# x also loaded turned, its first norm's factors applied after the product, and the first w_in slabs taken in a new order

## The chip, the cores and the metric

One Trainium2 chip, one core. The metric is the device time of one launch in microseconds. The kernel before takes 1186.05 us, the median of three runs (1185.82 to 1186.39).

## The reference

Two transformer blocks in a row on 512 tokens of width 1024, in float32. The change touches the start of the first: the first norm, the product with w_in, the norms of the heads.

```python
def rmsnorm(x, g):
    x32 = x.astype(jnp.float32)
    y = x32 * lax.rsqrt(jnp.mean(x32 * x32, axis=-1, keepdims=True) + EPS)
    return (y * g.astype(jnp.float32)).astype(x.dtype)
...
        xn = rmsnorm(x, attn_norm_g)
        proj = jnp.einsum('bsd,de->bse', xn, w_in)
        qa, ka, va, qb, kb, vb, f_logit = jnp.split(proj, IN_SPLITS, axis=-1)
        qa = rmsnorm(qa.reshape(b, s, A_HEADS, HEAD_DIM), q_norm_a)
        ka = rmsnorm(ka.reshape(b, s, A_KV_HEADS, HEAD_DIM), k_norm_a)
        out_a = swa_sinks_attention(qa, ka, va, sink_logits)
        ...
        out_b = forgetting_attention(qb, kb, vb, log_f)
        x = x + jnp.einsum('bse,ed->bsd', mixed, w_out)
        hn = rmsnorm(x, mlp_norm_g)
        hid = jnp.square(jax.nn.relu(jnp.einsum('bsd,df->bsf', hn, w_up)))
        x = x + jnp.einsum('bsf,fd->bsd', hid, w_down)
```

The second block (modulated norms, a pooling mixer, neighbourhood attention, a second MLP) follows and isn't changed.

## The kernel before

The code is written by engine: every engine's queue is an order set by hand, and semaphores join the queues. An engine does its instructions strictly in that order, so whatever stands behind a waiting one waits too.

**Products.** A float32 operand is split in a high part (rounded to fp32r) and a low part (the rest). A product is three matmuls for each of 8 blocks k of the inner dimension: high with high, high with low, low with high (`passes`, L1091 to L1093). xt_hi and xt_lo hold x turned: 128 partitions of the inner dimension, 8 blocks k, 512 tokens.

**Weights.** w_in is taken in five slabs (`IN1_COLS`): slab 0 is q of mixer a (512 columns), slab 1 its k and v and the forget logits (256 + 8 columns, in two loads, L512 and L513), slabs 2 to 4 are q, k, v of mixer b. A slab comes in four units q of two blocks k, 512 KB each, into raw[q] (the load on SP's queue, `unit`, L471); ScalarE writes the high part (`high`, L606), VectorE the low part (`low`, L1707), counted in hi_split and unit_split. A unit's load for the next slab waits until unit_split says that raw[q] was read. A slab's split also waits (`slab_end`) until the slab two before is used up.

**The start.** SP loads x tile 0 (128 tokens, 512 KB), unit 0 of slab 0, the identity, then units and x tiles in turn, then slab 1 with 17 small loads among it. TensorE spreads the norm's gain over the partitions by two products with a row of ones (L1148), then turns tile 0 of x times gain (`turn_half`, L1132, four turns each). The root of the mean square of tile 0 is late: it is applied behind the product (`root0`, `late_root`). Tiles 1 to 3 are scaled by root and gain first (`first_rows`, `scaled`, L1686), then turned; ScalarE copies the turns as xt_hi (`xt_high`, L636), VectorE subtracts for xt_lo (`xt_low`, L1697). ScalarE also does x's squares (`first_squares`, L620) and roots (`first_root`, L625, L626), VectorE the mean and refining (L1667, L1674, L1675).

**The order of tiles.** `FIRST` lists eight products (slab, row tile) g = 0 to 7 in the banks gp[g % 4]. `first_product` is the first, unit by unit; the others go through `product`, with turns put in their middle by `between(g)`. From g = 4 on a product waits until gp[g % 4] is free.

```python
FIRST = ((0, 0), (0, 1), (0, 2), (1, 0), (1, 1), (1, 2), (1, 3), (0, 3))
```

**The heads.** For each g: ScalarE squares the product (`head_squares`, L675), VectorE reduces it by heads (`head_means`, L1735, L1737), ScalarE takes two steps of the root (`head_roots`, L682, L683), VectorE refines it (`refine_heads`, L1660 to L1662) and writes the normed heads qn (`head_rows`, L1750 or L1751), which frees the bank (gemm_free). TensorE turns qn (`turn_heads`, L1207), and ScalarE stores q or k times gain (`head_gain`, L661, counted in qk_stored). For slab 1 ScalarE also copies v_a and flog (L718, L719). `sinks` (VectorE, L1776 to L1783) makes the sinks' rows from a small load.

**Behind it** runs a loop over `HALVES1` = 70 halves: attention of pairs of heads (`scores`, L1275; `maxima`, L1857; `exps`, L735; `turn_probs`; `copy_probs`; `values`) between three blocks k at a time of the products with slabs 2 to 4 (`part_product`). scores(0) waits for gemm_free 6, the small loads, the sinks and qk_stored 4 (k of tile 0); turn_probs(0), behind scores(1), waits for the exps of scores(0). Slab 2 is split by ScalarE around g = 6 and 7, since it takes the place of slab 1.

Of the kernel before, what the change touches and what calls it, by code (L numbers as in the profile page):

```python
# [14 lines left out]
P = 128  # L15
# [34 lines left out]
FIRST = ((0, 0), (0, 1), (0, 2), (1, 0), (1, 1), (1, 2), (1, 3), (0, 3))  # L50
N_IN1, N_OUT, N_MLP, N_IN2 = 5, 2, 4 * NCH, 4
# [188 lines left out]
def build(nc, t, out):  # L240
    ctx = ExitStack()
    with ctx:
# [50 lines left out]
        gain_row = at("gain_row", [1, D], F32, H + 28 * K)  # L293
        ones_row = at("ones_row", [1, P], F32, H + 20 * K)
# [37 lines left out]
        gains = place("gains", [P, 4], F32)  # L332
        cvec = place("cvec", [P, 2, KT], F32)
# [14 lines left out]
        gain1 = at("gain1", [P, D], F32, E)  # L348
# [38 lines left out]
        def sem(name):  # L387
# [70 lines left out]
        def _(sp):  # L458
# [5 lines left out]

            x_tile(0)
# [10 lines left out]
            def slab(s, w, c0, width):  # L476
                for q in range(UQ):
                    wait = 4 * (s - 1) + q + 1 if s else None
                    unit(q, rows(w, 0, q)[:, :, c0:c0 + width], width, wait)
                    if s == 0 and q == 0:  # L480
                        small(ident[:], t["c_ident"], ident_loaded)
                    if s == 0 and q:
                        x_tile(q)

            for s, (c0, width) in enumerate(IN1_COLS):
                if s == 1:

                    small_loads = (
                        (gains[0:HD, 0:1], t["q_norm_a"].rearrange("(p a) -> p a", a=1), heads_loaded),
                        (gains[HD:P, 0:1], t["q_norm_a"].rearrange("(p a) -> p a", a=1), heads_loaded),  # L490
                        (gains[0:HD, 1:2], t["k_norm_a"].rearrange("(p a) -> p a", a=1), heads_loaded),
                        (gains[HD:P, 1:2], t["k_norm_a"].rearrange("(p a) -> p a", a=1), heads_loaded),
                        (gains[0:HD, 2:3], t["q_norm_b"].rearrange("(p a) -> p a", a=1), heads_loaded),
                        (gains[HD:P, 2:3], t["q_norm_b"].rearrange("(p a) -> p a", a=1), heads_loaded),
                        (gains[0:HD, 3:4], t["k_norm_b"].rearrange("(p a) -> p a", a=1), heads_loaded),
                        (gains[HD:P, 3:4], t["k_norm_b"].rearrange("(p a) -> p a", a=1), heads_loaded),
                        (b_f[:], t["b_forget"].rearrange("(p a) -> p a", a=1), vec_loaded),
                        (sink[:], t["sink_logits"].rearrange("(a n) -> a n", a=1), vec_loaded),
                        (cvec[:, 0, :], t["c"], vec_loaded),
                        (cvec[:, 1, :], t["c_ctx"], vec_loaded),  # L500
                        (identb[:], t["c_identb"], vec_loaded),
                        (causal[:], t["c_causal"], vec_loaded),
                        (edge[:], t["c_edge"], vec_loaded),
# [3 lines left out]
                    for q in range(UQ):  # L507
                        src = rows(t["w_in"], 0, q)
                        for args in small_loads[5 * q:5 * (q + 1)]:
                            small(*args)  # L510
# [1934 lines left out]
```

## Time and profile before

| | |
|---|---|
| median of the runs | 1186.05 us (1185.82 to 1186.39) |
| the profiled execution | 1186.4 us, of which its span 1184.5 us |
| TensorE busy | 1167.0 us, 99% |
| VectorE, ScalarE, GpSimd busy | 706.3 us (60%), 476.1 us (40%), 24.8 us (2%) |
| TensorE clock granted | 0.998 of full speed, mean |
| DMA | 144.28 MB, mean 122 GB/s |

PE is TensorE's matmuls, PEld its weight loads, DVE is VectorE, ACT is ScalarE, SPq and ACTq are DMA issues by SyncE and ScalarE. A timeline's row gives the start in us from the span's start, the duration in us, engine, line, operation, tile written <- tiles read, shapes, count, and in square brackets how long the engine had been idle and what ended that. The ends of matmuls are modelled, so starts are what to read there. The chain of work that ended last is followed back from the last instruction.

### The profile page before, as it was taken

How to read it: one execution, taken by the hardware profiler on the slowest of the kernel's cores; microseconds unless marked ns; L12 is line 12 of the kernel's file. 1: busy time of each engine (PE TensorE's matmuls, PEld its weight loads, DVE VectorE, ACT ScalarE, POOL GpSimd, SP SyncE). 2: the span in 40 equal slices, each digit the busy share in tenths (PEclk: the TensorE clock that was granted, in tenths of full speed). 3: DMA queues.
4: the chain of work that ended last, by engine and by line, in shares of the span. 5: the costliest groups of instructions: out<-in, count | busy, mean ns of one | idle time of the engine just before them, and what ended most of it. 6: DMA issues, size and time to landing. Idle time of an engine off the chain costs nothing.

```text
span 1184.5 us, 16596 instructions
## 1 busy us (share of the span) xinstructions
PE 1167.0 (99%) x6158; PEld 946.1 (80%) x6160; DVE 706.3 (60%) x1084; ACT 476.1 (40%) x858; POOL 24.8 (2%) x23
## 2 busy tenths in 40 slices
PE   8999999989999999999999999999999999999997
PEld 5877776688888888888888886678988888888886
DVE  7786567768787786842788235747633333324335
ACT  6655344545234234324541114845631532432431
POOL 0000000000000000000000004300000000000000
PEclk9999999999999999999999999999999999999999
DMA  7322211218766676734425111222333322323301
GB/s 229 125 72 71 72 36 54 73 52 271 243 224 242 215 254 206 232 125 142 143 72 171 72 72 46 80 101 72 128 99 96 105 91 89 110 85 99 117 16 71
DMA packets 77533, 144.28 MB, mean 122 GB/s; under 512 B 8339, under 2 KB 12307, under 8 KB 77460
## 3 DMA queue, kind: packets, MB, share of 16 engines
q1 hardware_dynamic: 54882, 99.12, 24.7%
q10 hardware_dynamic: 22578, 44.18, 11.4%
q8 instruction: 46, 0.75, 0.3%
q14 instruction: 27, 0.22, 0.1%
HBM read 140.36 MB, written 2.13 MB: 120 GB/s over the span
## 4 chain that ended last, share of the span: by engine, by line
PE 91%; DVE 5%; ACT 2%; issue 2%; DMA 0%; DVEq 0%; ACTq 0%
PE gemm L1091 26%; PE gemm L1093 25%; PE gemm L1092 25%; PE aux L1132 1%; PE aux L1338 1%; PE gemm L1378 1%; PE gemm L1380 1%; PE gemm L1379 1%; DVE nmax L2199 1%; PE aux L1091 1%; PE gemm L1275 1%; PE aux L1093 1%; PE aux L1092 1%; PE gemm L1288 1%; PE aux L1617 1%
## 5 line engine op out<-in xcount | busy, mean ns | idle before, releaser
L1091 PE MATMUL gemm<-xt_hi,w_hi 128*128 128x512 f32 (+1 forms) x704 | 254.4, 361 | 1.3 <-issue 1.1
L1093 PE MATMUL gemm<-xt_hi,w_lo 128*128 128x512 f32 (+1 forms) x704 | 253.6, 360 | 0.0
L1092 PE MATMUL gemm<-xt_lo,w_hi 128*128 128x512 f32 (+1 forms) x704 | 253.5, 360 | 0.0
L1707 DVE TENSOR_TENSOR w_lo<-w_raw,w_hi 128x1024 fp32r<-128x1024 f32 (+1 forms) x176 | 208.0, 1210 | 35.1 <-ACT w_hi L842 30.4
L842 ACT ACTIVATE w_hi<-w_raw 128x1024 fp32r<-128x1024 f32 x124 | 124.1, 1050 | 211.4 <-PE gemm L1093 132.9
L1091 PE MATMUL gemm<-w_hi,ht_hi 128*128 128x512 f32 (+1 forms) x512 | 198.9, 388 | 0.0
L1093 PE MATMUL gemm<-w_hi,ht_lo 128*128 128x512 f32 (+1 forms) x512 | 198.4, 387 | 0.0
L1092 PE MATMUL gemm<-w_lo,ht_hi 128*128 128x512 f32 (+1 forms) x512 | 198.4, 387 | 0.0
L1091 PEld LDWEIGHTS gemm<-xt_hi,w_hi 128*128 128x128 f32 x704 | 132.7, 188 | 21.9 <-issue 1.7
L1093 PEld LDWEIGHTS gemm<-xt_hi,w_lo 128*128 128x128 f32 x704 | 132.7, 189 | 20.1
L1092 PEld LDWEIGHTS gemm<-xt_lo,w_hi 128*128 128x128 f32 x704 | 132.7, 188 | 19.8
L2005 DVE TENSOR_TENSOR ht_lo<-hid,ht_hi 128x512 fp32r<-128x512 f32 x64 | 44.3, 692 | 162.4 <-ACT hid L855 162.4
L1093 PEld LDWEIGHTS gemm<-w_hi,ht_lo 128*128 128x128 f32 x512 | 96.1, 188 | 19.7
L1092 PEld LDWEIGHTS gemm<-w_lo,ht_hi 128*128 128x128 f32 x512 | 96.2, 188 | 19.5
L1091 PEld LDWEIGHTS gemm<-w_hi,ht_hi 128*128 128x128 f32 x512 | 96.1, 188 | 19.4
L850 ACT ACTIVATE relu<-gemm 128x512 f32<-128x512 f32 x64 | 38.2, 597 | 165.3 <-PE gemm L1093 160.2
L2062 DVE SCALAR_TENSOR_TENSOR mod_acc<-wm,csil,mod_acc 128x512 f32<-128x512 f32 x112 | 84.1, 751 | 5.8 <-DMA wm<-in_w_mod 1.5
L1091 PE MATMUL gemm<-w_hi,xt_hi 128*128 128x512 f32 (+1 forms) x208 | 80.2, 386 | 0.4 <-DVE xt_lo L1697 0.4
L1093 PE MATMUL gemm<-w_hi,xt_lo 128*128 128x512 f32 (+1 forms) x208 | 77.9, 374 | 0.0
L1092 PE MATMUL gemm<-w_lo,xt_hi 128*128 128x512 f32 (+1 forms) x208 | 77.6, 373 | 0.0
L606 ACT ACTIVATE w_hi<-w_raw 128x1024 fp32r<-128x1024 f32 (+1 forms) x52 | 51.0, 1021 | 61.1 <-PE gemm L1093 60.0
L2019 DVE TENSOR_TENSOR sub<-sub,gemm 128x512 f32<-128x512 f32 (+1 forms) x24 | 16.2, 676 | 60.5 <-PE gemm L1093 60.5
(268 smaller groups left out, 1385.8 us busy)
## 6 DMA issues: line engine op xcount, KB each, us to landing
wm<-in_w_mod ACTq DMA_DIRECT2D x64, 512.0 KB, 4.7
w_raw<-in_w_in SPq DMA_DIRECT2D x32, 512.0 KB, 4.3
w_raw<-in_w_up SPq DMA_DIRECT2D x32, 512.0 KB, 3.9
w_raw<-in_w_down SPq DMA_DIRECT2D x32, 512.0 KB, 5.7
w_raw<-in_w_mlp_in SPq DMA_DIRECT2D x32, 512.0 KB, 3.6
w_raw<-in_w_mlp_out SPq DMA_DIRECT2D x32, 512.0 KB, 4.4
w_raw<-in_w_out SPq DMA_DIRECT2D x16, 512.0 KB, 4.0
x<-in_x SPq DMA_DIRECT2D x4, 512.0 KB, 6.5
```

The lines of the kernel that those rows point to most:

```text
L606: act.activation(w_hi[slot(s)][:, UK * q:UK * (q + 1), 0:width], raw[q][:, :, 0:width], ACT.Copy).then_inc(hi_split, 1)
L842: act.activation(w_hi[s % 2][:, UK * q:UK * (q + 1), :], raw[q][:, :, :], ACT.Copy).then_inc(hi_split, 1)
L850: act.activation(relu[c % 2][:], gp[(t0 + c) % 4][:], ACT.Relu).then_inc(relu_done, 1)
L1091: pe.matmul(bank, lh, rh, start=(k == 0), stop=False)
L1092: pe.matmul(bank, lh, rl, start=False, stop=False)
L1093: mm = pe.matmul(bank, ll, rh, start=False, stop=(k == KT - 1))
L1132: mm = pe.transpose(dst, src, ident[:])
L1275: pe.matmul(bank[e][:, lo:256], q_a[rows[e], h // 2, n * P:(n + 1) * P], k_a[rows[e], swap, (n - 1) * P + lo:(n + 1) * P], start=True, sto ...
L1707: dve.tensor_tensor(w_lo[slot(s)][:, ks, 0:width], raw[q][:, :, 0:width], w_hi[slot(s)][:, ks, 0:width].bitcast(F32), ALU.subtract).then_i ...
L2005: dve.tensor_tensor(ht_lo[:, c, :], hid[c % 2][:], ht_hi[:, c, :].bitcast(F32), ALU.subtract).then_inc(hid_lo, 1)
L2019: dve.tensor_tensor(cols, cols, bank[:], ALU.add).then_inc(gemm_free, 1)
L2062: ins = dve.scalar_tensor_tensor(acc, w, c, acc, ALU.mult, ALU.add)
```

## The change

The host lays x out once more, turned (`x_turned`, 8 blocks k of 128 partitions x 512 tokens), the norm's gain by partition, the head gains in one array and the two conditioning vectors in one. In the kernel:

- The gain products, the turns of x and `first_rows` are gone. ScalarE issues the load of the gain and five loads of x_turned (blocks 0 and 1 singly, then three units) and writes xt_hi as x_turned times gain for all 512 tokens (`x_high`); VectorE writes the low part from the same (`x_low`). All four row tiles have the root applied behind the product (`root1`): in head_squares, v_a, flog, the heads' norm and v_b.
- Slab 0's unit 0 is loaded and split by single blocks k. `first_products` runs tiles 0, 1 and 2 of slab 0 together, unit by unit; in the last unit tile by tile.
- SP loads slab 0, then x tile q and slab 1's unit q in turn, then seven small loads, slab 2, three small loads, and the rest as before.
- x's squares, roots and refining, and the split of slab 1, stand behind slab 0's split on ScalarE and VectorE; head_squares(0) waits for all four roots. The alibi load is issued ahead of the heads.
- head_gain and turn_heads of tile u run at g = u + 4 instead of u + 3; sinks stands behind tile 4 instead of tile 1.

```diff
+FIRST_ROWS = 3
...
-        gain_row = at("gain_row", [1, D], F32, H + 28 * K)
-        ones_row = at("ones_row", [1, P], F32, H + 20 * K)
+        x_turned = at("x_turned", [P, KT, S], F32, H)
...
-        root0 = st[:, 3, STAT_N1:STAT_N1 + 1]
-
-        def late_root(m):
-            return {"scale": root0} if m == 0 else {}
+        def root1(m):
+            return st[:, 3, STAT_N1 + m:STAT_N1 + m + 1]
...
+            def first_unit():
+
+                c0, width = IN1_COLS[0]
+                for k in range(UK):
+                    sp.dma_start(raw[0][:, k, 0:width], t["w_in"][k * P:(k + 1) * P, c0:c0 + width]
+                                 ).then_inc(first_loaded if k == 0 else raw_loaded[0], 16)
+
+            first_unit()
+            for q in range(1, UQ):
+                unit(q, rows(t["w_in"], 0, q)[:, :, IN1_COLS[0][0]:IN1_COLS[0][0] + IN1_COLS[0][1]], IN1_COLS[0][1], None)
+            for q in range(UQ):
+                x_tile(q)
+                src, c0 = rows(t["w_in"], 0, q), IN1_COLS[1][0]
+                sp.wait_ge(unit_split, q + 1)
+                sp.dma_start(raw[q][:, :, 0:256], src[:, :, c0:c0 + 256]).then_inc(raw_loaded[q], 16)
+                sp.dma_start(raw[q][:, :, 256:KV_W], src[:, :, 2304:2312]).then_inc(raw_loaded[q], 16)
+            small(gains[:], t["head_gains"], heads_loaded)
+            small(ident[:], t["c_ident"], ident_loaded)
...
+            slab(2, t["w_in"], *IN1_COLS[2])
+            small(edge[:], t["c_edge"], vec_loaded)
+            small(pscale[:], t["pool_scale"], vec_loaded)
+            small(negsel[:].rearrange("h g p -> h (g p)"), t["c_negsel"], negsel_loaded)
...
-            load(gain_row[:], t["attn_norm_g"].rearrange("(a n) -> a n", a=1), gain1_loaded)
+            load(gain1[:], t["attn_norm_g"], gain1_loaded)
+            for k in range(UK):
+                load(x_turned[:, k, :], t["x_turned"][:, k, :], first_turned if k == 0 else turned_loaded[0])
+            for q in range(1, UQ):
+                load(x_turned[:, UK * q:UK * (q + 1), :], t["x_turned"][:, UK * q:UK * (q + 1), :], turned_loaded[q])
...
+            def x_high(k):
+
+                act.wait_ge(*x_arrived(k))
+                did(act.activation(xt_hi[:, k, :], x_turned[:, k, :], ACT.Copy, scale=gain1[:, k:k + 1]), xt_hi_done)
+
+            act.wait_ge(gain1_loaded, 16)
+            x_high(0)
+            act.wait_ge(first_loaded, 16)
+            act.activation(w_hi[slot(0)][:, 0, :], raw[0][:, 0, :], ACT.Copy).then_inc(first_split, 1)
+            x_high(1)
+            act.wait_ge(raw_loaded[0], 16)
+            act.activation(w_hi[slot(0)][:, 1, :], raw[0][:, 1, :], ACT.Copy).then_inc(hi_split, 1)
+            for q in range(1, UQ):
+                x_high(UK * q)
+                x_high(UK * q + 1)
+                high_of(0, q)
+            for m in range(TT):
+                first_squares(m)
+                if m:
+                    first_root(STAT_N1 + m - 1)
+                high_of(1, m)
+            first_root(STAT_N1 + TT - 1)
...
                 if g == 0:
-                    act.wait_ge(rs_done, 4)
+                    act.wait_ge(rs_done, 2 * TT)
                 did(act.activation(qsq[:, 0:heads * HD], banks[in_bank(g)][:, 0:heads * HD], ACT.Square,
-                                   **late_root(m)), hsq_done)
+                                   scale=root1(m)), hsq_done)
...
-            act.wait_ge(heads_loaded, 16 * 8)
-
-            for g, (s, m) in list(enumerate(FIRST))[2:]:
-                if g >= 3:
-                    head_gain(g - 3)
+            for g, (s, m) in enumerate(FIRST):
+                if g == 4:
+                    act.wait_ge(heads_loaded, 16)
+                if g >= 4:
+                    head_gain(g - 4)
...
+            head_gain(4)
...
+            def first_products():
+
+
+                def step(m, k, lhs, w):
+                    return pe.matmul(gp[m][:], lhs[:, k, m * P:(m + 1) * P], w[slot(0)][:, k, :],
+                                     start=(lhs is xt_hi and w is w_hi and k == 0), stop=(w is w_lo and k == KT - 1))
...
-                if g < TT - 1:
-                    turn_rows(NT_1 + g + 1)
-                if g >= 3:
-                    if g == 3:
-                        pe.wait_ge(xt_lo_done, 2 * TT)
-                    turn_heads(g - 3)
+                if g == 4:
+                    pe.wait_ge(ident_loaded, 16)
+                if g >= 4:
+                    turn_heads(g - 4)
+
+            first_products()
+            split_ready(1)
...
+            turn_heads(4)
...
+            def x_low(k):
+
+                dve.wait_ge(*x_arrived(k))
+                dve.wait_ge(xt_hi_done, k + 1)
+                did(dve.scalar_tensor_tensor(xt_lo[:, k, :], x_turned[:, k, :], gain1[:, k:k + 1],
+                                             xt_hi[:, k, :].bitcast(F32), ALU.mult, ALU.subtract), xt_lo_done)
...
+            for m in range(TT):
+                mean_square(STAT_N1 + m, STAT_N1 + m + 1)
+                if m:
+                    refine(STAT_N1 + m - 1)
+                low(1, m)
+            refine(STAT_N1 + TT - 1)
...
+            for g in range(PHASE - 1):
                 head_means(g)
...
                 head_rows(g)
+                if g == 4:
+                    sinks()
```

## Rows read from the trace of the kernel before

**Rows 1.** The page: TensorE's busy time, and the chain that ended last.

```profile
PE 1167.0 (99%) x6158; PEld 946.1 (80%) x6160; DVE 706.3 (60%) x1084; ACT 476.1 (40%) x858; POOL 24.8 (2%) x23
...
PE 91%; DVE 5%; ACT 2%; issue 2%; DMA 0%; DVEq 0%; ACTq 0%
```

**Rows 2.** The timeline of TensorE: start, duration, engine, line, operation, tiles, shapes.

```profile
3.34 3.75 PE L1148 MATMUL gemm<-gain_row,ones_row 1*128 1x512 f32 x4 [3.34 <-DMA gain_row<-in_attn_norm_g]
...
8.87 1.92 PE L1162 MATMUL gemm<-w_hi,xt_hi 128*128 128x512 f32 x4
...
22.48 0.40 PE L1091 MATMUL gemm<-w_hi,xt_hi 128*128 128x512 f32 x1
22.71 0.39 PE L1092 MATMUL gemm<-w_lo,xt_hi 128*128 128x512 f32 x1
...
37.04 0.60 PE L1207 MATMUL aux<-ident,qn 128*128 128x128 f32 x4
...
40.38 0.60 PE L1207 MATMUL aux<-ident,qn 128*128 128x128 f32 x4
...
51.20 0.49 PE L1275 MATMUL gemm<-k_a,q_a 64*128 64x128 f32 x4
...
56.57 0.49 PE L1275 MATMUL gemm<-k_a,q_a 64*128 64x128 f32 x4
...
246.36 0.66 PE L1132 MATMUL aux<-ident,xr 128*128 128x128 f32 x4 [1.99 <-DVE xt_lo L1697]
```

**Rows 3.** Stretches of the start: busy time by engine, clock, DMA share, GB/s.

```profile
5.00:10.00 5.00, 5.00 (x14) 2.30 (x12) 4.05 (x6) 3.89 (x8) 0.00 (x0) 1.00 1.03 369
...
15.00:20.00 5.00, 4.48 (x22) 3.04 (x21) 4.72 (x10) 4.12 (x9) 0.00 (x0) 1.00 0.72 173
```

**Rows 4.** The line that loads x, on SP's queue: issues and time to landing.

```profile
L463 SPq DMA_DIRECT2D x<-in_x x4: 396/470/523, 0.7 to 5.5; - x4
...
DMA to landing us min/median/max: 3.8/6.5/9.0
```

**Rows 5.** The timeline of ScalarE (ACT; ACTq is its DMA issues).

```profile
9.82 0.58 ACT L636 ACTIVATE xt_hi<-aux 128x512 fp32r<-128x512 f32 x1
10.43 1.06 ACT L620 ACTIVATE junk<-x 128x1024 bf16<-128x1024 f32 x1
...
11.61 1.06 ACT L606 ACTIVATE w_hi<-w_raw 128x1024 fp32r<-128x1024 f32 x1
...
13.19 0.20 ACT L625 ACTIVATE st<-st 128x1 f32<-128x1 f32 x1
...
18.24 1.18 ACT L606 ACTIVATE w_hi<-w_raw 128x528 fp32r<-128x528 f32 x2
...
32.38 0.37 ACTq L593 DMA_DIRECT2D alibi<-in_c_alibi  x1
...
49.11 0.47 ACT L661 ACTIVATE k_a<-aux,gains 128x256 f32<-128x256 f32 x1
```

**Rows 6.** The timeline of VectorE (DVE): a row tile scaled by root and gain.

```profile
14.41 1.28 DVE L1686 SCALAR_TENSOR_TENSOR xr<-x,st,gain 128x1024 f32<-128x1024 f32 x1
```

**Rows 7.** The same: sinks, and the reduces that begin each tile's head norm.

```profile
33.78 0.16 DVE L1776 CAST sink_parts<-sink 1x8 bf16<-1x8 f32 x1
...
35.45 0.69 DVE L1735 TENSOR_REDUCE hst<-qsq 128x8 f32<-128x512 f32 x1
...
38.32 0.28 DVE L1735 TENSOR_REDUCE hst<-qsq 128x2 f32<-128x128 f32 x1
...
41.17 0.29 DVE L1735 TENSOR_REDUCE hst<-qsq 128x2 f32<-128x128 f32 x1 [0.25 <-ACT qsq L675]
...
46.30 0.29 DVE L1735 TENSOR_REDUCE hst<-qsq 128x2 f32<-128x128 f32 x1
...
53.18 0.68 DVE L1735 TENSOR_REDUCE hst<-qsq 128x8 f32<-128x512 f32 x1
```

**Rows 8.** The timeline of ScalarE: the end of the first pair's exps.

```profile
55.40 0.19 ACT L735 ACTIVATION_READ_ACCUMULATOR prob_a<-gemm,nmax 128x1 f32 x1
```

More of the change, by code:

```diff
@@ L479, in slab @@
                     unit(q, rows(w, 0, q)[:, :, c0:c0 + width], width, wait)
[L480 to L503, printed above, removed]
-                        (pscale[:], t["pool_scale"], vec_loaded),
-                        (negsel[:].rearrange("h g p -> h (g p)"), t["c_negsel"], negsel_loaded),
-                    )
[L507 to L510, printed above, removed]
-                        sp.wait_ge(unit_split, q + 1)
-                        sp.dma_start(raw[q][:, :, 0:256], src[:, :, c0:c0 + 256]).then_inc(raw_loaded[q], 16)
-                        sp.dma_start(raw[q][:, :, 256:KV_W], src[:, :, 2304:2312]).then_inc(raw_loaded[q], 16)
-                else:
-                    slab(s, t["w_in"], c0, width)
@@ L516, in _ @@
+            small(edge[:], t["c_edge"], vec_loaded)
+            small(pscale[:], t["pool_scale"], vec_loaded)
+            small(negsel[:].rearrange("h g p -> h (g p)"), t["c_negsel"], negsel_loaded)
+            for s, (c0, width) in list(enumerate(IN1_COLS))[3:]:
+                slab(s, t["w_in"], c0, width)
             for half in range(2):
@@ L717, in _ @@
                 if s == 1:
-                    did(act.activation(v_a[:, m, :], gp[g % 4][:, P:2 * P], ACT.Copy, **late_root(m)), v_copied)
-                    did(act.activation(flog[:, m, :], gp[g % 4][:, 256:KV_W], ACT.Copy, **late_root(m)), v_copied)
+                    did(act.activation(v_a[:, m, :], gp[g % 4][:, P:2 * P], ACT.Copy, scale=root1(m)), v_copied)
+                    did(act.activation(flog[:, m, :], gp[g % 4][:, 256:KV_W], ACT.Copy, scale=root1(m)), v_copied)
+            head_gain(4)
             def exps(p):
@@ L1142, in turn_rows @@
                     turn_half(n, half, permute)
-            pe.wait_ge(row_ready, 1)
-            pe.wait_ge(gain1_loaded, 16)
-            for half in range(2):
-                pe.matmul(gp[2 + half][:], ones_row[:], gain_row[:, half * NC:(half + 1) * NC],
-                          start=True, stop=True).then_inc(gain_spread, 1)
-            pe.wait_ge(ident_loaded, 16)
-            pe.wait_ge(first_half, 1)
-            turn_half(NT_1, 0)
-            pe.wait_ge(xr_ready, NT_1 + 1)
-            turn_half(NT_1, 1)
@@ L1748, in norm @@
                 def norm(dst, src, scale):
-                    if m == 0:
-                        return dve.scalar_tensor_tensor(dst, src, root0, scale, ALU.mult, ALU.mult)
-                    return dve.tensor_tensor(dst, src, scale, ALU.mult)
+                    return dve.scalar_tensor_tensor(dst, src, root1(m), scale, ALU.mult, ALU.mult)
                 if g >= 2:
```

224 lines of the change are left out of this document (95 added, 129 removed).

## The prediction

> **What bounds the kernel now.** I read the page first: TensorE is busy 99% of the span and the chain that ended last lies on it for 91% [rows 1], so time comes off only where TensorE waits, or where work leaves it. Then the timeline of TensorE, for its waits and its milestones. It idles 3.3 us before the first instruction (for the gain row) and under 2 us in all while the first tiles are made; from 21 us on it doesn't wait until 246.36 [rows 2]. The milestones: first matmul 3.34, first real product 8.87, first attention scores 51.20, second scores 56.57 [rows 2]. The change ends before the first scores, so the question is how much earlier the scores can start, and that is asked of three other queues: the loads [rows 3, 4], ScalarE [rows 5, 8] and VectorE [rows 6, 7]. In the kernel before they run beside TensorE with about 1 us to spare: the second scores (56.57) need the exps of the first, which ended at 55.40 + 0.19 = 55.6 [rows 2, 8].
>
> **What leaves TensorE.** Two gain products (four passes, 3.75 us [rows 2]) and 32 row turns, some 4 us in four rounds. Three row tiles of slab 0 are 72 matmuls at a spacing of 22.71 - 22.48 = 0.23 us [rows 2], 16.4 us, as before. A tile of slab 1 with its head turns is 40.38 - 37.04 = 3.3 us, unchanged.
>
> **TensorE's new start.** The first piece (xt k=0, w k=0, 256 KB each) has to land, and be rounded twice by ScalarE. A 512 KB x tile landed 3.8 us after its issue at the earliest [rows 4]; half as much, with the second queue beside it and an issue at 1.3 us (the gain load goes first), I put at 4.4. Two roundings of 128x512 at 0.6 us (9.82 to 10.43 [rows 5]; its source is PSUM, the nearest row) give 5.65. The first products of before began at 8.87 with four in 1.92 us and some waiting between [rows 2], nearer 0.43 apart than 0.23, which is the 1.2 GHz level, after 5.5 us of light work. If the new ones are at that level until about 9.7 us, unit 0 ends at 11.7; the rest is at 0.23, and the third tile is done at 24.0 (25 at the outside, 23 if never slow). None of these ends anything, as the next parts show. VectorE keeps up: x_low is new, 512 columns of a scalar_tensor_tensor, between half of the 1.28 us that 1024 columns took [rows 6] and 0.75, so a unit is at most 2 x 0.75 + 1.2 = 2.7 us of VectorE against 18 x 0.23 = 4.1 of TensorE.
>
> **The loads.** x_turned and slab 0 are 4.2 MB, as x and slab 0 were before. There the last of them was issued at 5.55 and landed 9.0 us later, 14.55 [rows 4]; in between the engines moved 369 GB/s at a busy share of 1.03 [rows 3]. The identity's 64 KB is no longer ahead: 14.3 for the last unit. Unit 1 lands at 8.7, unit 2 at 11.5. Behind them on SP's queue stand x in rows (4 x 512 KB) and slab 1's pieces. Between 15 and 20 us, with such short rows in flight, the engines moved 173 GB/s at a share of 0.72, which is 240 at a full share [rows 3]. x tile 0 lands 0.52 MB / 369 = 1.4 us later, 15.7. Behind it 1.57 MB of x and 0.81 MB of slab 1 precede x tile 3's end: all at 369 it is 22.2, all at 240 it is 25.6. x has rows of 4 KB as unit loads of 369 had, so I take 369 for x and 300, between the two, for slab 1: 22.6.
> By the Trainium skill (DMA: Bandwidth & Descriptors, Specifications) the fabric gives up to 435 GB/s; by that the last unit would be there some 2 us sooner. The trace's 369 over a saturated stretch speaks against it.
>
> **ScalarE's queue, the first half of the new path.** Unit 3 lands at 14.3; two xt roundings (0.61 each) and one w rounding (0.97 from start to start [rows 5]) end at 16.5. Behind these stand, moved, all of x's statistics: four squares at 1.18 (10.43 to 11.61), four roots at 0.46 (13.19, 0.20, and its pair, with the steps between), and four slab-1 roundings at 0.54 (18.24, two in 1.18 with their overlap) [rows 5]. That is 8.7 us, with gaps 8.8: 25.3, squares 1 to 3 finding their x tiles by 18.0, 20.3 and 22.6 where they want them at 18.3, 20.5 and 22.7. The alibi load is issued before the head squares now; that costs ScalarE 0.37 us and the gaps around it, 0.5 (32.38 [rows 5]): 25.8. VectorE's last refine ends at 26.0 (its low part of slab 1 goes first). head_squares(0) waits for it, takes 0.7, and the first head reduce starts at 26.8. TensorE's slab 1 can start at 25.5 (split_ready), 1.5 us after its tile 2.
>
> **The heads' chain, the second half.** Per tile it is reduce, mean, ScalarE roots, refine, norm: 38.32 - 35.45 = 2.87 us for 512 columns, 41.17 - 38.32 = 2.85 for slab 1's first [rows 7]. Now every tile has the late root: the norm is a scalar_tensor_tensor (0.06 dearer), each ScalarE read of the product has a scale (0.09 dearer). Three tiles at 2.93: 35.6. Tile 3, 2.95: 38.55. Tile 4's own steps are 2.5, then sinks, 35.45 - 33.78 = 1.7 [rows 7], which is moved behind it: 42.75. Tile 5, 2.9: 45.65, against 46.30 before [rows 7]. From there to the reduce of tile 7 it took 53.18 - 46.30 = 6.9 [rows 7], now 7.05 with the dearer forms: 52.7, half a microsecond earlier than before. maxima(0) is next on VectorE. On ScalarE head_gain(4), 0.5 us, now stands between head_roots(7) and the first exps. Before, the exps ended 55.6 - 53.18 = 2.4 after that reduce; now 2.9: 55.6.
>
> **TensorE against that chain.** Tile 4 of FIRST needs gp[0] free (29.7), so TensorE stands 1.2 us there; tiles 4 to 7 are then 3 x 3.3 + 5.8, ending at 45.6 with the last turn, 5.6 us ahead of before (51.20). The first scores need qk_stored 4. Before, head_gain(3) was done long ahead; now it stands on ScalarE behind the squares of tile 6 (45.6), two roundings of slab 2 (1.9), roots (0.5), v_a and flog (0.7), itself 0.5 (the k gain at 49.11 [rows 5]): 49.2. So TensorE idles 3.6 us there, and what it queues behind scores(0) (tile 8's product, turn_heads(5)) waits too. Second scores: wanted at 49.2 + 5.4 = 54.6, exps there at 55.6, another 1.0 idle.
>
> **Sum.** Second scores at 55.6 instead of 56.57: 1.0 us. From there TensorE had no wait, and the next deadlines keep over 0.7 us: exps(1) end near 59.6 for scores(2) wanted at 61.6. The extra 0.06 to 0.09 per norm and square of tiles 8 to 15 lie beside it and cost nothing while that cover holds; without it at most 8 x 0.15 = 1.2 us. The small loads behind slab 1 and slab 2 are issued by 28 us, sinks wants them at 41; slab 2's four units land by 31, wanted at 45: nothing. The profiled execution took 1186.4, 1.9 over its span; less 1.0 is 1185.4; the median of the runs lies 0.35 under the profiled one: 1185.1.
>
> **Rivals.**
> *Slower: x's rows come late.* Place: the squares on ScalarE before the heads' chain. It decides once x tile 3 lands after 22.7 us; from there each us is one on the whole path. At 240 GB/s (25.6) it costs 2.9: 1188.0. At 173 GB/s [rows 3], the far end, the 2.4 MB take 13.8 us, x tile 3 lands at 29.5, 6.8 late: 1191.9. For it: the spare is under 0.4 us at every tile. Against: two thirds of the bytes are x's long rows, and that stretch's queue wasn't full. Chance 0.15, half of it beyond 0.2%.
> *The clock falls.* TensorE stands 3.6 us at the first scores. After 1.99 us of idling at 246 us its four turns took 0.66 us, the upper level [rows 2]; 3.6 us no row shows. If the scores and twelve matmuls behind them ran at 1.2 GHz (0.43 for 0.23), they would take 3 more, less 1.0 of spare: 1187.1. The Trainium skill (TensorE: Matmul & The Clock Gate, Part 1) holds that idling is what puts the array back to its lower level. Chance 0.10.
> *Faster: the loads are no bound.* ScalarE's own work before the squares, 8 x 0.61 + 1.2 + 3 x 0.97 = 9.0 from 4.4, would end at 13.4 instead of 16.5: 3 us more off, 1182.1. Against: 369 GB/s is all that was moved at a full share. Chance 0.12.
> *Faster: TensorE's own count.* Who reads only that TensorE is the chain takes 51.2 - 45.6 = 5.6 off: 1180.5. It needs the heads' chain to be 5 us quicker than its rows. Chance 0.10.
>
> **How the numbers follow.** Forecast 0.53, the rivals 0.15, 0.10, 0.12, 0.10. 0.2% is 2.4 us, about what a measurement of this kernel can tell from no change. Faster: the two fast rivals and a little of the forecast's own spread (its 45 small steps, 1.5 us either way), 0.25. Slower: half the first rival and a bit of the second, 0.10. Same 0.65. The range leaves out the last rival and the far end of the first, past 240 GB/s: 1181.8 to 1188.2.
>
> **What would show it.** Right: the first reduce of heads near 26.8; the last x_low unit's data near 14.3; TensorE idle over 3 us before scores(0), released by ScalarE's k_a gain; the second scores near 55.6, released by ScalarE's exps. Wrong: ScalarE's squares released by x loads (first rival); matmul spacing of 0.43 after the idle (second); ScalarE busy without gaps before 14 us (third); scores(0) before 47 us (fourth). Also wrong: a new wait of TensorE after 60 us.

## The result, and the profile after

| | before | changed |
|---|---|---|
| median of 15 runs each, one chip | 1185.93 us (1185.36 to 1186.42) | 1188.17 us (1187.49 to 1188.78) |
| ratio | | 1.0019, 95% interval 1.0011 to 1.0026 |
| span of the profiled execution | 1184.5 us | 1186.5 us |
| TensorE busy | 1167.0 us | 1162.7 us |
| TensorE clock granted, mean | 0.998 | 0.996 |
| second scores start | 56.57 us | 58.60 us |

The changed kernel is slower by 2.2 us (1.3 to 3.1 by the interval). The forecast was 1185.1, a microsecond faster; the time lies at the upper edge of the range. TensorE has 4.3 us less to do and is done 2 us later. The page of the changed kernel (TensorE's busy time, and the chain that ended last), against [rows 1]:

```profile
PE 1162.7 (98%) x6124; PEld 945.4 (80%) x6124; DVE 702.4 (59%) x1078; ACT 478.3 (40%) x858; POOL 24.7 (2%) x23
...
PE 89%; DVE 5%; ACT 3%; issue 2%; DMA 1%; ACTq 0%; DVEq 0%
```

Still TensorE's chain, but two points of it have gone over to ScalarE and DMA. Where, its timeline tells (the columns are those of [rows 2]):

```profile
7.01 1.62 PE L1141 MATMUL gemm<-w_hi,xt_hi 128*128 128x512 f32 x3 [7.01 <-ACT w_hi L649]
...
46.68 0.38 PE L1204 MATMUL aux<-ident,qn 128*128 128x128 f32 x2
50.42 0.80 PE L1268 MATMUL gemm<-k_a,q_a 64*128 64x128 f32 x4 [3.36 <-ACT k_a L669]
...
53.00 0.63 PE L1083 MATMUL gemm<-w_hi,xt_hi 128*128 128x512 f32 x1
...
58.60 0.49 PE L1268 MATMUL gemm<-k_a,q_a 64*128 64x128 f32 x4
...
248.53 0.66 PE L1124 MATMUL aux<-ident,xr 128*128 128x128 f32 x4 [2.02 <-DVE xt_lo L1689]
```

Read against [rows 2]: TensorE's work of the start ends near 47.0, where before it went on to the first scores at 51.20; the first scores (50.42) are 0.8 ahead; the second (58.60) are 2.03 late, and so is the row at 248.53 (2.17). The whole loss arises between 50.42 and 58.60: scores to scores is 8.18 us where it was 5.37. Behind 50.42 TensorE has no wait, and yet a matmul has 0.63 for 0.39 and they are 0.43 apart instead of 0.23. TensorE's share of that stretch by windows (start and end, length, busy, count, granted clock as a share of full speed, DMA share, GB/s):

```profile
47.00:49.00 2.00, 0.06 (x1) 1.00 0.00 0
49.00:50.50 1.50, 0.08 (x2) 0.70 0.24 27
50.50:52.00 1.50, 1.50 (x9) 0.50 0.91 317
...
54.00:56.00 2.00, 2.00 (x8) 0.50 0.80 220
56.00:58.00 2.00, 2.00 (x9) 0.89 0.79 294
```

While TensorE idles the granted clock goes to 0.50, which is 1.2 GHz of 2.4 (the row from 49 us), and it comes back after 56, when TensorE has been busy since 50.42.

ScalarE's timeline, the other half (answers to [rows 5, 8]):

```profile
5.48 0.72 ACT L644 ACTIVATE xt_hi<-x_turned,gain 128x512 fp32r<-128x512 f32 x1 [3.45 <-DMA x_turned<-in_x_turned]
...
7.73 0.72 ACT L644 ACTIVATE xt_hi<-x_turned,gain 128x512 fp32r<-128x512 f32 x1 [0.86 <-DMA x_turned<-in_x_turned]
...
9.88 1.48 ACT L644 ACTIVATE xt_hi<-x_turned,gain 128x512 fp32r<-128x512 f32 x2 [0.76 <-DMA x_turned<-in_x_turned]
...
17.29 1.04 ACT L618 ACTIVATE junk<-x 128x1024 bf16<-128x1024 f32 x1
...
26.93 0.69 ACT L683 ACTIVATE qsq<-gemm,st 128x512 f32<-128x512 f32 x1 [0.95 <-DVE st L1667]
...
49.80 0.47 ACT L669 ACTIVATE k_a<-aux,gains 128x256 f32<-128x256 f32 x1
...
56.54 0.19 ACT L727 ACTIVATION_READ_ACCUMULATOR prob_a<-gemm,nmax 128x1 f32 x1
```

From 9.88 on ScalarE waits for no load. The exps that the second scores need end at 56.73, 1.1 us behind the forecast's 55.6. VectorE's reduces at the head norm's beginning (answers to [rows 7]):

```profile
27.73 0.69 DVE L1734 TENSOR_REDUCE hst<-qsq 128x8 f32<-128x512 f32 x1 [0.89 <-ACT qsq L683]
...
53.81 0.68 DVE L1734 TENSOR_REDUCE hst<-qsq 128x8 f32<-128x512 f32 x1
```

So two things have to be told apart: a chain that is 1.1 us later than forecast, and 58.60 - 56.73 = 1.9 us behind it. The theory for the second: TensorE's idle of 3.36 us lowered its clock, and the matmuls between the two scores, at 1.2 GHz, outlast the chain. The rival: the chain alone sets the second scores, and the low clock is hidden beside it.

### The profile page after: what moved, and what is told of

It reads as the page before. It is cut to its first block, busy times and chain, and to the rows that moved or that the text cites. A ratio compares the mean times of both kernels' runs of the same rounds, so it can differ in the third digit from the quotient of the medians.

```text
span 1186.5 us, 16514 instructions
## 1 busy us (share of the span) xinstructions
PE 1162.7 (98%) x6124; PEld 945.4 (80%) x6124; DVE 702.4 (59%) x1078; ACT 478.3 (40%) x858; POOL 24.7 (2%) x23
## 3 DMA queue, kind: packets, MB, share of 16 engines
q10 hardware_dynamic: 23440, 46.28, 11.8%
## 4 chain that ended last, share of the span: by engine, by line
PE 89%; DVE 5%; ACT 3%; issue 2%; DMA 1%; ACTq 0%; DVEq 0%
PE gemm L1083 25%; PE gemm L1084 25%; PE gemm L1085 25%; PE aux L1331 1%; PE aux L1124 1%; PE gemm L1371 1%; PE aux L1578 1%; PE aux L1610 1%; PE gemm L1373 1%; PE gemm L1372 1%; PE aux L1083 1%; PE gemm L1268 1%; PE aux L1085 1%; PE aux L1084 1%; PE gemm L1281 1%
## 5 line engine op out<-in xcount | busy, mean ns | idle before, releaser
L1083 PE MATMUL gemm<-w_hi,xt_hi 128*128 128x512 f32 (+1 forms) x192 | 75.0, 391 | 1.7 <-DVE qn L1748 1.1
L1085 PE MATMUL gemm<-w_hi,xt_lo 128*128 128x512 f32 (+1 forms) x192 | 72.3, 377 | 0.0
L1084 PE MATMUL gemm<-w_lo,xt_hi 128*128 128x512 f32 (+1 forms) x192 | 72.2, 376 | 0.0
```

Source lines behind the costliest of these rows:

```text
L1083: pe.matmul(bank, lh, rh, start=(k == 0), stop=False)
L1084: pe.matmul(bank, lh, rl, start=False, stop=False)
L1085: mm = pe.matmul(bank, ll, rh, start=False, stop=(k == KT - 1))
```

## The experiments

The changed kernel's median minus that of the kernel before, on one chip, is +2.2 us. Beside the experiments the kernel before ran on their chip, with medians of 1186.43 us (e1 to e4), 1186.51 (e5 to e8), 1186.24 (e9 to e12) and 1186.37 (e13); every ratio is to that.

**e1_fill14 and e2_fill4_mid: keep TensorE busy there.** Dummy matmuls whose product is overwritten, in the changed kernel.

```diff
             turn_heads(4)
+            for _ in range(14):
+                pe.matmul(gp[0][:], xt_hi[:, 0, 0:P], xt_hi[:, 0, :], start=True, stop=True)
```

e2_fill4_mid has 4 of them behind `pe.wait_ge(hi_split, 10)`, slab 2's unit 1.

> The changed kernel with 14 extra matmuls (xt_hi with xt_hi, into gp[0], read by nobody) right behind turn_heads(4), so that TensorE has something to do while it waits for scores(0); no other queue is touched. They take 14 x 0.23 = 3.2 us of the 3.36 us wait. Theory CLOCK (the wait lets TensorE's clock fall to 1.2 GHz, and the slow stretch behind it is the loss): granted clock 1.00 from 45 to 60 us, the second scores start when ScalarE's exps are done, 56.8 instead of 58.6, time 1.8 us under the changed kernel, about 1186.3, 0.2 to 0.4 over before. Rival CHAIN (the loss is the later chain of heads and exps, the slow clock only fills waiting time): the second scores and the time stay as in the changed kernel, 1188.2.

> The changed kernel with only 4 extra matmuls behind turn_heads(4), which wait for the second high part of slab 2 (hi_split 10, about 48.7 us), so that the 3.36 us wait is cut into two of about 1.9 and 0.8 us. If the fall of the clock needs the long wait in one piece, it stays away as with 14: 1186.3. If it is the sum of idle time around there that counts, the clock still falls: 1188. CHAIN: 1188.2.

e1_fill14: 1187.10 us, ratio 1.0008 (0.9999 to 1.0017); e2_fill4_mid: 1187.06, 1.0012 (1.0003 to 1.0021). TensorE's timeline of e1_fill14:

```profile
50.68 0.49 PE L1270 MATMUL gemm<-k_a,q_a 64*128 64x128 f32 x4 [0.16 <-ACT k_a L669]
...
57.02 0.49 PE L1270 MATMUL gemm<-k_a,q_a 64*128 64x128 f32 x4 [0.38 <-ACT prob_a L727]
```

and of e2_fill4_mid, its idle cut in two:

```profile
49.08 1.19 PE L1223 MATMUL gemm<-xt_hi 128*128 128x512 f32 x4 [1.74 <-ACT w_hi L604]
50.71 0.49 PE L1271 MATMUL gemm<-k_a,q_a 64*128 64x128 f32 x4 [0.44 <-ACT k_a L669]
...
57.06 0.49 PE L1271 MATMUL gemm<-k_a,q_a 64*128 64x128 f32 x4 [0.39 <-ACT prob_a L727]
```

In both profiled executions the clock stays at 1.00, the scores(0) matmuls have 0.49 for 0.80, and the second scores are now released by ScalarE's exps, as the forecast had it. By the medians more work on TensorE makes the kernel a microsecond faster (the ratios' intervals, 1.0011 to 1.0026 and 0.9999 to 1.0017, overlap a little; the second scores don't, nor do the spans, 1184.6 to 1185.2 us in e1's eleven executions and 1185.7 to 1187.0 in the changed kernel's fifteen). Theory CLOCK had 1186.3, 0.8 lower. The clock's part of the loss is 58.60 - 57.02 = 1.6 us of the span; what is left, 57.02 - 56.57 = 0.45, is the chain. In this execution x's first pieces landed later, and the first reduce is at 27.97 for 27.73; with that 0.24 taken off, the clock's part is 1.8 us, near the 1.9 of above.

**e3_gain_first: remove the idle by order.** head_gain(3), which scores(0) waits for, goes ahead of slab 2's two roundings on ScalarE.

```diff
-                if g >= 4:
+                if 4 <= g < 7:
                     head_gain(g - 4)
...
                 if g == 6:
+                    head_gain(3)
                     high_of(2, 0)
                     high_of(2, 1)
```

> The changed kernel with head_gain(3) moved on ScalarE from behind the roots and copies of tile 6 to directly behind its squares, ahead of slab 2's first two splits. scores(0) can start at about 47.3 instead of 50.4. The splits, and with them the chain of heads, come 0.5 us later: exps of the first pair done at 57.2. CLOCK: no idle stretch over 3 us is left before scores(0); TensorE then waits about 1.5 us for slab 2's low part, 0.5 at the third unit and 2.5 before the second scores; the clock stays up and the second scores start at 57.3 instead of 58.6: 1186.9. CHAIN (a later chain costs as much as before): 0.5 us over the changed kernel, 1188.7.

1188.59 us, ratio 1.0021 (1.0012 to 1.0030): nothing won. That is the number of rival CHAIN (1188.7), but not by its cause. Its timeline on TensorE:

```profile
47.64 0.49 PE L1269 MATMUL gemm<-k_a,q_a 64*128 64x128 f32 x4 [0.31 <-ACT k_a L669]
...
52.34 0.63 PE L1084 MATMUL gemm<-w_hi,xt_hi 128*128 128x512 f32 x1 [3.96 <-DVE qn L1749]
...
58.70 0.49 PE L1269 MATMUL gemm<-k_a,q_a 64*128 64x128 f32 x4
```

scores(0) came 2.8 us earlier, and the next instruction in TensorE's queue, tile 8's product, then waited 3.96 us for head_rows(6) on VectorE. The idle had moved by one instruction and lowered the clock just the same. The wait I had overlooked is the one queued behind the waiting instruction.

**e4_stats_spread: shorten the chain.** The squares and roots of tiles 2 and 3 leave the front of the chain and go among heads 0 and 1; head_squares(0) waits for tile 0's and 1's alone.

```diff
+                if g in (0, 2, 6):
+                    act.wait_ge(rs_done, {0: 2, 2: 8, 6: 11}[g])
                 head_squares(g)
+                if g < 2:
+                    first_squares(g + 2)
...
                 head_roots(g)
+                if g < 2:
+                    first_root(STAT_N1 + g + 2)
```

VectorE's mean and refine steps of these tiles move alike, and the alibi load is issued at g = 2.

> The changed kernel with the statistics of x spread: on ScalarE only tiles 0 and 1 are squared ahead of slab 1's split, head_squares(0) waits for tile 0's root alone, and squares, roots and refining of tiles 2 and 3 go between the heads of tiles 0 and 1; the alibi load goes behind them. The first reduce of heads then starts when the first product is done, about 24.0 instead of 27.7 us. The chain ends 3.5 to 3.8 us sooner: exps of the first pair done at 53.0 instead of 56.7; scores(0) at 46.6, an idle stretch of 1.6 us before it and 1.1 before the second scores, no fall of the clock. Both CLOCK and CHAIN expect a gain, CLOCK 5.6 us (second scores at 53.0 instead of 58.6: 1182.6, 3.4 under before), CHAIN 3.7 (1184.5).

1185.28 us, ratio 0.9991 (0.9982 to 1.0001). ScalarE's and TensorE's timelines:

```profile
23.83 0.65 ACT L604 ACTIVATE w_hi<-w_raw 128x528 fp32r<-128x528 f32 x1 [1.27 <-DMA w_raw<-in_w_in]
```

```profile
48.64 0.49 PE L1274 MATMUL gemm<-k_a,q_a 64*128 64x128 f32 x4 [3.72 <-ACT k_a L671]
...
56.09 0.49 PE L1274 MATMUL gemm<-k_a,q_a 64*128 64x128 f32 x4
```

The first reduce came at 25.14, 2.6 us earlier (a load took the place of the last microsecond, the 1.27 above), and the exps ended at 54.94. The second scores stand 1.15 behind that: the clock fell again after the 3.72 us. Of the 2.6 us only 1.8 reached the exps, since the moved squares lengthen the heads' chain (first to last reduce 26.88 us for 26.08). Both theories had expected more (1182.6 and 1184.5). So the chain and the clock are two losses, and each can be had back alone.

**e5_spread_fill and e6_sinks_in_gaps: both at once.** e5 is e4 with e2's dummies. e6 moves besides the sinks' nine small VectorE operations from one block behind head_rows(4), where they take 1.7 us of the chain, into the gaps where VectorE waits for ScalarE's roots.

```diff
+                if g in (3, 4, 5):
+                    sinks(g - 3)
                 head_rows(g)
-                if g == 4:
-                    sinks()
```

> The kernel changed, with tiles 2 and 3's statistics spread among the heads (as in e4_stats_spread) and four dummy matmuls behind turn_heads(4) that wait for slab 2's unit 1 (as in e2_fill4_mid). Theory (two losses that add up: the heads' chain sets the second scores, and TensorE's 3.7 us of idling ahead of scores(0) lowers its clock): the granted clock stays at 1.00 from 47 to 58 us, the second scores start when the second pair of exps is ready, at 54.9 to 55.1 (e4_stats_spread 56.09, the kernel before 56.57), the span is 1183.0 and the median 1184.1 to 1184.6. Rival (what TensorE does at 1.2 GHz is hidden behind the chain once the chain ends earlier): second scores at 56.0 as in e4_stats_spread, median 1185.3.

> e5_spread_fill, with the sinks' nine small VectorE operations not in one block behind head_rows(4) but three each between head_means(g) and head_rows(g) for g = 3, 4 and 5, where VectorE waits for ScalarE's roots. Theory (the heads' chain sets the second scores, and the block lies on it with some 1.3 us): head reduces of tiles 5 to 7 come 0.9 to 1.3 us earlier than in e5_spread_fill, second scores at 53.8 to 54.2, median 1183.0 to 1183.8. Rival (another wait is late next: TensorE's product of tile 8 behind gemm_free 7, or ScalarE's high parts of slab 2): reduces earlier but second scores within 0.3 us of e5_spread_fill's, median the same.

e5: 1184.92 us, ratio 0.9989 (0.9980 to 0.9998), but not as expected: with the chain earlier, slab 2's unit had become the late one, so that the dummies stood behind an idle of their own. Its timeline:

```profile
47.02 1.20 PE L1229 MATMUL gemm<-xt_hi 128*128 128x512 f32 x4 [2.16 <-ACT w_hi L604]
...
55.71 0.49 PE L1277 MATMUL gemm<-k_a,q_a 64*128 64x128 f32 x4
```

and by windows its clock fell just the same (0.50 from 49 to 52 us). e6: **1183.34 us, ratio 0.9974 (0.9963 to 0.9984)**, faster than both kernels. Its timeline on TensorE, and its first and last head reduce on VectorE:

```profile
45.24 1.19 PE L1229 MATMUL gemm<-xt_hi 128*128 128x512 f32 x4
46.88 0.49 PE L1277 MATMUL gemm<-k_a,q_a 64*128 64x128 f32 x4 [0.44 <-ACT k_a L671]
...
53.23 0.49 PE L1277 MATMUL gemm<-k_a,q_a 64*128 64x128 f32 x4 [0.36 <-ACT prob_a L733]
```

```profile
24.66 0.68 DVE L1745 TENSOR_REDUCE hst<-qsq 128x8 f32<-128x512 f32 x1
...
50.25 0.68 DVE L1745 TENSOR_REDUCE hst<-qsq 128x8 f32<-128x512 f32 x1
```

The last reduce is 1.77 earlier than in e5 (52.02), the clock stays at 1.00, the second scores are 3.34 us ahead of before, and the span is shorter by as much (1181.2 for 1184.5). Not all of the 1.77 is the move's: e5's first reduce is at 25.11 and e6's at 24.66, since x's pieces landed later in e5's execution (the first one was taken up at 5.85 us, in e6 at 5.54). From first to last reduce it is 26.91 in e5 and 25.59 here, so the move is worth 1.3, the upper end of what was expected.

**e7_pause8, e8_pause_short and e12_pause5: the idle alone.** The kernel before, where nothing but a pause is added ahead of scores(0): GpSimd waits for tile 7's product and clears a pad sixteen, eight or five times.

```diff
+            pool.wait_ge(gemm_done, 8)
+            for i in range(16):
+                pool.memset(pad[:], 0.0).then_inc(pad_done, 1)
+                pool.wait_ge(pad_done, i + 1)
...
                     pe.wait_ge(silu_step, SINK_STEPS)
+                    pe.wait_ge(pad_done, 16)
```

> The kernel before, with a pause alone: GpSimd waits for tile 7's product, clears a small pad sixteen times, and scores(0) waits for the last of these, so that TensorE idles D us there, and nothing else is changed. D should be near 4 us. Theory (an idle of this length in front of scores(0) lowers the clock, and what follows at half the clock costs extra): granted clock 0.5 for some 5 us behind the pause, second scores at 56.57 + D + 1.8 to 2.8, span 1184.5 + D + 1.8 to 2.8. Rival (the low clock in the kernel changed comes from something else of its start, not from the idle): clock 1.00, second scores and span + D alone.

> The same with eight clears, D near 2 us. Theory (idles of 1.7 to 2.0 us in e2_fill4_mid and e1_fill14's neighbourhood left the clock at 1.00): clock stays 1.00, second scores and span + D alone. Rival (any idle of 2 us or more lowers it): D + 1.8 or more, with clock 0.5 behind it.

> The kernel before, with the pause of five clears, an idle of some 1.5 to 1.7 us in front of scores(0). Theory (an idle has to be longer than some 2 us here before the clock is lowered): clock 1.00 from 51 to 60 us, second scores and span + D alone. Rival (each pause lowers it, as the 2.36 us did): D + 1.7, clock 0.5 behind it.

They gave 1192.84 us (ratio 1.0057, 1.0041 to 1.0072), 1190.39 (1.0030, 1.0020 to 1.0041) and 1187.83 (1.0016, 1.0007 to 1.0026). TensorE's timeline of e7_pause8 (sixteen), then of e8_pause_short (eight), then of e12_pause5 (five):

```profile
55.63 0.80 PE L1282 MATMUL gemm<-k_a,q_a 64*128 64x128 f32 x4 [4.46 <-POOL pad L566]
...
62.47 0.49 PE L1282 MATMUL gemm<-k_a,q_a 64*128 64x128 f32 x4
```

```profile
53.74 0.49 PE L1282 MATMUL gemm<-k_a,q_a 64*128 64x128 f32 x4 [2.36 <-POOL pad L566]
...
60.65 0.49 PE L1282 MATMUL gemm<-k_a,q_a 64*128 64x128 f32 x4
```

```profile
52.00 0.49 PE L1282 MATMUL gemm<-k_a,q_a 64*128 64x128 f32 x4 [1.57 <-POOL pad L566]
...
57.38 0.49 PE L1282 MATMUL gemm<-k_a,q_a 64*128 64x128 f32 x4
```

Scores to scores is 6.84, 6.91 and 5.38 us, where before it is 5.37. In the profiled executions the pauses of 4.46 and 2.36 cost 1.5 us beyond their own length each, with the clock at 0.50 in the windows behind them; the one of 1.57 cost only itself. With nothing of the change in these kernels, the idle of 4.46 is shown as a sufficient cause. The shorter ones don't decide alone, as the spans of the other executions tell. e12's ten spans are seven from 1185.1 to 1186.2 us and three of 1187.7 to 1187.9, so that 1.57 us probably lowered the clock too in three of them; e8's eight go from 1187.1 to 1188.9, and 1187.1, with a mean granted clock of 0.999, is about the pause itself over before. Two sizes of mine fell: the extra cost is 1.5, not 1.8 to 2.8, and an idle of 2.4 us is not safe. The changed kernel lost more between the two scores, 2.8 us (8.18 for 5.37): its clock was low from before 50.42 to about 56, in e7 only up to 59 behind scores at 55.63.

**e9_plain_x: the price of the scale.** e2_fill4_mid, but this kernel leaves the gain out of x's high part.

```diff
-                did(act.activation(xt_hi[:, k, :], x_turned[:, k, :], ACT.Copy, scale=gain1[:, k:k + 1]), xt_hi_done)
+                did(act.activation(xt_hi[:, k, :], x_turned[:, k, :], ACT.Copy), xt_hi_done)
```

> e2_fill4_mid, with x's high part taken by ScalarE without the norm's gain as a scale (the gain is left out of the high part, so the output's values are others). Theory (the high part of x costs 0.72 to 0.75 us because of the scale that is read per partition, where the prediction took 0.61, and ScalarE's queue sets the first head reduce): the high part costs 0.58 to 0.63 us, no wait for x takes its place from the third pair on, the first square starts at 16.4 to 16.8 us (17.29 in the kernel changed), the first head reduce at 26.9 to 27.3 (27.73) and the second scores at 56.1 to 56.5 (57.06). Rival (x's rows, not ScalarE, set the pace in the first 17 us): the high parts get shorter but waits for x_turned grow by the same, first square at 17.2, second scores at 57.0.

Its timeline on ScalarE:

```profile
7.98 0.63 ACT L644 ACTIVATE xt_hi<-x_turned 128x512 fp32r<-128x512 f32 x1 [1.19 <-DMA x_turned<-in_x_turned]
...
16.89 1.04 ACT L618 ACTIVATE junk<-x 128x1024 bf16<-128x1024 f32 x1
```

A block takes 0.63 for 0.72. Against e2_fill4_mid, which it differs from by this alone, the first square is at 16.89 for 17.55 and the first reduce at 27.34 for 28.01. ScalarE's last wait for x ends at 10.04 (in e2 at 10.14), and from there to the first square it is 6.85 us for 7.41: 0.56 of the 0.67 is the scale, 0.1 a load. Up to there the rival is right, since what a shorter block saves is waited away (1.19 us for the second block, 1.08 in e2). The time says nothing (1186.96, ratio 1.0006, 0.9997 to 1.0015), because in this profiled execution the clock fell, where e2_fill4_mid's had kept it. TensorE's timeline of e9_plain_x:

```profile
48.41 1.21 PE L1223 MATMUL gemm<-xt_hi 128*128 128x512 f32 x4 [1.74 <-ACT w_hi L604]
50.04 0.49 PE L1271 MATMUL gemm<-k_a,q_a 64*128 64x128 f32 x4 [0.41 <-ACT k_a L669]
...
57.48 0.49 PE L1271 MATMUL gemm<-k_a,q_a 64*128 64x128 f32 x4
```

The same two idles as in e2_fill4_mid to 0.03 us, and the other outcome.

**e10_sinks_alone and e11_before_sinks: whose gain is it?** The sinks' move alone, in the changed kernel and in the one before.

> The kernel changed, with the sinks' nine small operations in the gaps of heads 3, 4 and 5 and nothing else (no dummy matmuls, statistics as changed). Theory (the heads' chain is late, and TensorE's idle ahead of scores(0) is what remains until tile 6's k_a): the reduces of tiles 5 to 7 come 1.4 to 1.8 us earlier than in the kernel changed, scores(0) starts at 48.7 after an idle of 1.6 to 2.0 us, the clock stays at 1.00 (the idle of 1.74 us left it there, the one of 2.16 did not), second scores at 55.0 to 55.4, median 1184.6 to 1185.3. Rival (an idle of under 2 us can lower the clock as well): scores(0) at the same time, clock 0.5 behind it, second scores at 56.3 or later, median 1186 or more.

> The kernel before, with the same move of the sinks' operations alone. Theory (there TensorE works without a wait up to the second scores, so the heads' chain is covered and the gain of e6_sinks_in_gaps needs the change): head reduces of tiles 5 to 7 earlier, second scores at 56.5 to 56.6 as before, median within 0.5 us of the kernel before. Rival (the gain is the move's own and no part of the change): second scores a microsecond earlier or more, median 1185 or less.

e10: 1185.96 us, ratio 0.9997 (0.9988 to 1.0006). Its timeline:

```profile
49.23 0.49 PE L1268 MATMUL gemm<-k_a,q_a 64*128 64x128 f32 x4 [2.03 <-ACT k_a L669]
...
56.42 0.49 PE L1268 MATMUL gemm<-k_a,q_a 64*128 64x128 f32 x4
```

The clock fell after 2.03 us, as its rival had it. The chain is shorter by 1.35 us (first to last reduce 24.73 for 26.08), below the 1.4 to 1.8 expected. Even so this one move gives the change's loss of 2.2 us back, within the interval. e11: 1186.58 us, ratio 1.0001 (0.9992 to 1.0010), second scores at 56.44 as before: there TensorE's own work covers the chain, and the move is worth nothing. The gain of e6 is one that the change makes possible.

**e13_no_dummies: does the best version need its dummies?**

> e6_sinks_in_gaps without the four dummy matmuls: the kernel changed, with tiles 2 and 3's statistics among the heads and the sinks' operations in the gaps. TensorE then idles from the last head turn's end, 45.2 us, to scores(0) at 46.9, 1.6 to 1.7 us at a stretch, as in e12_pause5 (1.57, clock kept). Theory (the two moves of small work carry the gain, and with an idle this short the clock is kept most times): clock 1.00 behind scores(0), second scores at 53.2 to 53.6, median 1183.3 to 1184.0. Rival (the gain needs the dummies, because with the idle the clock falls): clock 0.5 for some microseconds behind scores(0), second scores at 54.5 to 55.0, median 1185 or more.

1183.77 us, ratio 0.9975 (0.9963 to 0.9986), the same as e6 within the intervals. Its profile shows a longer idle than I had expected, and the fall:

```profile
47.05 0.49 PE L1274 MATMUL gemm<-k_a,q_a 64*128 64x128 f32 x4 [2.41 <-ACT k_a L671]
...
54.58 0.49 PE L1274 MATMUL gemm<-k_a,q_a 64*128 64x128 f32 x4
```

The gain is the shorter chain's. The idle probably takes a part of it back in some executions: the spans of its seven are 1180.5, 1180.6, 1181.3 and four from 1182.0 to 1182.5. But e6's eight, with the dummies, go from 1180.6 to 1182.5 too, so what the dummies add isn't shown.

## Why the prediction was wrong, step by step

- **The milestone.** Right: the second scores carried the result to the end (+2.03 there, +2.0 in the span; in e6 -3.34 and -3.3).
- **TensorE's new start.** Wrong in size, harmless: first piece rounded from 5.48, not 4.4; first matmul 7.01, not 5.65; tile 2's last matmuls near 25.8, not 24.0. Nothing waited for it.
- **The loads.** The mechanism was wrong. I let the last unit's landing (14.3) hold ScalarE up; it waited for no load after 9.88. When the last unit landed no row shows; ScalarE began on it at 14.82, in e9 at 14.61, without a wait. The early pieces were later than forecast (unit 1 9.88 for 8.7). The DMA engines moved more than the 369 GB/s of [rows 3], by the windows of the changed kernel:

```profile
5.00:10.00 5.00, 2.99 (x7) 2.44 (x8) 2.85 (x4) 2.83 (x5) 0.00 (x0) 1.00 1.03 401
10.00:15.00 5.00, 5.00 (x19) 3.99 (x19) 3.96 (x6) 4.87 (x7) 0.00 (x0) 1.00 1.04 399
```

  x in rows was never late, so the first rival (*x's rows come late*) didn't come true.
- **ScalarE's queue.** The term that was mis-sized: x's high part at 0.61 a block, taken from a plain rounding in [rows 5], was 0.72 alone and 0.74 in pairs. The same text had added 0.09 for a per-partition scale to the heads' reads and forgotten it here. The first two blocks don't count, since ScalarE waits for x behind each of them. From 9.88 on six blocks and three roundings of w_in take 7.41 us without a gap, and at 0.61 a block they would have taken 6.6: the first square would have stood at 16.5, as forecast, but by luck, since the forecast got there by the loads. It is at 17.29, 0.8 late. What stands behind it was sized right (17.29 to 25.98 is 8.7; 8.8 was forecast). First reduce 27.73 for 26.8. By e9_plain_x the scale costs 0.09 to 0.10 a block and 0.56 us of the 0.8; the rest is that without a scale a block took 0.66 from start to start there, and not the 0.61 of [rows 5], whose source is PSUM. The Trainium skill (ScalarE: Activation LUTs, What ACT_TABLE_LOAD costs) puts a per-partition pointer operand at about 93 ns; the trace agrees.
- **The heads' chain.** Right: 26.8 to 52.7 was forecast as 25.9 us, measured 53.81 - 27.73 = 26.08. The sinks' block was in the sum, and I didn't ask whether it had to be; in the gaps it gives back 1.3 us (e6, e10).
- **TensorE against that chain.** Right in its place and its releaser: an idle of 3.36 us (3.6 forecast) for ScalarE's k_a. **This is the step that failed**: it left TensorE's clock at its upper level behind the idle, and so put what the idle costs the matmuls behind it at nothing. The only row near, 1.99 us at 246 [rows 2], was shorter, and its four turns couldn't have told: they take 0.65 or 0.66 us in all 15 profiled kernels, also in the five where the clock falls, because it falls behind them. I gave the rival *The clock falls* 0.10. It came true, with its price: 3 us less 1.0 of spare is 2.0; measured 1.9 (granted clock 0.50, second scores 1.9 us behind the exps, and right behind them with the idle filled, e1).
- **The sum.** 1185.1, and 1.1 for the later chain, and 1.9 for the clock, is 1188.1; measured 1188.17. The 1.1 is 0.8 up to the first square, 0.1 to the first reduce and 0.2 to the last; the landing of x's pieces moves it by up to 0.3 between executions (first reduce 27.73 here, 27.97 to 28.01 in e1 to e3).
- **The third rival** (*the loads are no bound*) had half of its premise fulfilled, no wait for loads behind 9.88, and still not its time: its 9.0 us of ScalarE's work from 4.4 were 11.8 from 5.48, 1.6 of them waiting. The *TensorE's own count* rival needed scores(0) before 47; they came at 50.42.

## What to carry to other kernels

When a change takes work off the bound engine, ask where that engine will idle instead and for how long: an idle of TensorE of 2 us or more has to be priced with the matmuls behind it at half the clock, here 1.5 to 1.9 us beyond its length, and a shorter one with a part of that. An engine freed by 4 us gives nothing while the chain that feeds it stays as long; the gain beyond the kernel before came when that chain's statistics moved off its front and its small work into its gaps (e6, e13), and the move into the gaps was worth nothing in the kernel before (e11). Before moving one awaited instruction forward, read what waits next in the same queue (e3).

## What the runs showed of the hardware that was not expected

**The same idle, two outcomes.** In the profiled executions idles about the first scores of 2.03, 2.16, 2.36, 2.41, 3.36, 3.72, 3.96 and 4.46 us were each followed by a stretch at 0.50; one of 1.57 us wasn't; 1.74 + 0.4 us was in e9_plain_x and wasn't in e2_fill4_mid. One kernel's executions differ as well (e8 and e12 above). Near 246 us (243 to 252) all of the 15 profiled kernels have an idle of 1.99 to 2.03 us for VectorE's xt_lo. In ten of them, the kernel before among them, the clock stays; in five (e2, e5, e7, e10, e11) it falls. TensorE from 248 to 254 us, of the kernel before and then of e11_before_sinks, which is the same there:

```profile
248.00:254.00 6.00, 4.95 (x35) 1.00 0.28 87
```

```profile
248.00:254.00 6.00, 6.00 (x33) 0.76 0.28 87
```

So the row on which the forecast rested its upper level showed one draw of two. The Trainium skill (TensorE: Matmul & The Clock Gate, Part 1: The HAM clock gate) says that the gate keeps its own time and isn't reset when a kernel starts; by that one idle can fall either way, and the two outcomes agree. No run here shows the mechanism itself.

**The clock at the start.** The first matmuls of the changed kernel (7.01 to about 12) are 0.43 us apart, the spacing of 1.2 GHz, while the windows' granted clock reads 1.00 for 5 to 15 us. Ahead of them TensorE had done nothing. From about 12.2 on they are 0.23 apart. At the start it is the spacing that has to be read.

**The rate of the loads.** With x_turned issued by ScalarE and slab 0 by SP, 399 to 401 GB/s were moved from 5 to 15 us, where [rows 3] had 369 for nearly the same bytes, x and slab 0 both issued by SP. That the queue is the reason wasn't tried, and the kernel before speaks against it: with SP alone its DMA engines moved 409 from 10 to 12 us.

```profile
10.00:12.00 2.00, 2.00 (x9) 1.00 1.04 409
```

So the forecast's 369 wasn't all that is moved at a full share. It was the mean of 5 to 10 us, and the same trace had more to show 2 us on.
